# The inverse in an RWKV chunk loop: one factor by products, the other by 32x32 turns on VectorE

## What is computed

```python
def step(S, inp):
    r_t, w_t, k_t, v_t, kk_t, b_t = inp
    sa = jnp.einsum('bhvk,bhk->bhv', S, kk_t)
    S = (S * w_t[:, :, None, :] - sa[..., None] * b_t[:, :, None, :]
         + v_t[..., None] * k_t[:, :, None, :])
    return S, jnp.einsum('bhvk,bhk->bhv', S, r_t)
...
for d, reverse in enumerate((False, True)):
    ...
    yd_c, s_ctx = rwkv_scan(r_c, dec_c, k_c, v_c, kk_c, a_c, s0, reverse)
    yd, _ = rwkv_scan(r, dec, k_d, v, kk, a_d, s_ctx, reverse)
```

## Time and profile before

| | us |
|---|---|
| runs of the kernel before | 2665.66, 2661.81, 2665.49 |
| median | 2665.49 |
| profiled execution, its own time | 2672.74 |
| its span | 2671.0 |
| TensorE busy in the span | 2488.5 |
| VectorE / ScalarE / GpSimd busy | 1335.5 / 512.6 / 141.3 |

### The profile page before, as it was taken

The page is one execution under the profiler, slowest core; times in us unless marked ns, Lnnn a source line. Parts: engine busy times, 40 slices in busy tenths (PEclk is TensorE's granted clock), DMA queues, the critical chain, the costliest instruction groups (busy, mean ns, idle before and its releaser), DMA issues.

```text
span 2671.0 us, 49291 instructions
## 1 busy us (share of the span) xinstructions
PE 2488.5 (93%) x21560; PEld 1925.8 (72%) x21560; DVE 1335.5 (50%) x2478; ACT 512.6 (19%) x1032; POOL 141.3 (5%) x106
## 2 busy tenths in 40 slices
PE   8989999999999999999998989988887798999997
PEld 5945888888686548888884755457777746888786
DVE  4535555533454336555432365545665436787533
ACT  2122100101003320100001043323343222212100
POOL 0000000000000000000000000003223200000000
PEclk9988999999999999999999989998999998999998
DMA  5323322233221023222235102100000023222132
GB/s 165 119 79 126 95 71 88 75 87 107 64 66 62 1 77 113 95 79 70 77 93 160 48 16 66 51 1 4 5 4 4 4 95 119 71 95 95 48 88 71
DMA packets 221181, 190.53 MB, mean 71 GB/s; under 512 B 8727, under 2 KB 219064, under 8 KB 220968
## 3 DMA queue, kind: packets, MB, share of 16 engines
q1 hardware_dynamic: 220674, 187.29, 22.8%
q10 hardware_dynamic: 294, 0.09, 0.0%
HBM read 185.25 MB, written 2.10 MB: 70 GB/s over the span
## 4 chain that ended last, share of the span: by engine, by line
PE 86%; DVE 5%; issue 4%; ACT 1%; SPq 1%; POOL 1%; DMA 1%; DVEq 0%; POOLq 0%; ACTq 0%
PE psum L1630 30%; PE psum L1840 14%; PE psum L512 9%; PE psum L1130 4%; PE psum L2680 4%; PE psum L1344 3%; PE psum L2673 3%; PE psum L1341 3%; PE psum L3237 2%; PE psum L542 2%; PE psum L1066 1%; PE psum L2270 1%; PE psum L2252 1%; PE psum L1109 1%; PE psum L534 1%
## 5 line engine op out<-in xcount | busy, mean ns | idle before, releaser
L1630 PE MATMUL psum<-sbuf 128*128 128x256 f32 x3696 | 804.3, 381 | 4.0 <-DVE sbuf L476 1.9
L1630 PEld LDWEIGHTS psum<-sbuf 128*128 128x128 f32 x3696 | 704.7, 191 | 103.3 <-issue 3.2
L1840 PE MATMUL psum<-sbuf 128*128 128x256 f32 x1848 | 405.2, 382 | 11.1 <-DVE sbuf L1858 5.5
L1840 PEld LDWEIGHTS psum<-sbuf 128*128 128x128 f32 x1848 | 353.8, 192 | 62.1 <-DVE sbuf L1858 6.3
L1714 DVE TENSOR_TENSOR sbuf<-sbuf,psum 128x256 f32<-128x256 f32 x462 | 177.9, 417 | 200.5 <-PE psum L1630 199.3
L512 PE MATMUL psum<-sbuf 128*128 128x512 f32 (+3 forms) x688 | 248.1, 519 | 4.3 <-DVEq L617 4.0
L2680 PE MATMUL psum<-sbuf 64*64 64x64 f32 x4992 | 196.6, 225 | 40.3 <-issue 24.7
L512 PEld LDWEIGHTS psum<-sbuf 128*128 128x128 f32 (+2 forms) x688 | 129.6, 190 | 115.6 <-issue 103.4
L2680 PEld LDWEIGHTS psum<-sbuf 64*64 64x64 f32 x4992 | 170.6, 136 | 52.8 <-issue 43.9
L2673 PE MATMUL psum<-sbuf 64*64 64x64 f32 (+1 forms) x4544 | 176.1, 229 | 24.1 <-issue 17.9
L2673 PEld LDWEIGHTS psum<-sbuf 64*64 64x64 f32 x4544 | 158.6, 137 | 30.7 <-issue 21.5
(11 more groups left out here) (280 smaller groups left out, 2684.7 us busy)
## 6 DMA issues: line engine op xcount, KB each, us to landing
sbuf<-in_w_mod_dram SPq DMA_DIRECT2D x24, 1024.0 KB, 5.2
sbuf<-in_w_ffn_gate_dram SPq DMA_DIRECT2D x22, 1024.0 KB, 5.5
sbuf<-in_w_ffn_up_dram SPq DMA_DIRECT2D x22, 1024.0 KB, 7.6
sbuf<-in_w_ffn_down_dram SPq DMA_DIRECT2D x32, 704.0 KB, 6.0
sbuf<-in_w_up_dram SPq DMA_DIRECT2D x22, 1024.0 KB, 7.2
sbuf<-in_w_out_dram SPq DMA_DIRECT2D x12, 1024.0 KB, 8.1
sbuf<-in_w_in_dram SPq DMA_DIRECT2D x12, 1024.0 KB, 5.5
sbuf<-in_w_down_dram SPq DMA_DIRECT2D x16, 704.0 KB, 6.1
```

What stands on the lines that cost most here:

```text
L1630: mm = pe.matmul(bank, w[:, q, :], rhs[:, q, :], start=q == 0, stop=q == 3)
L1840: mm = pe.matmul(bank_of(g, p), wt[:, q, :], rhs_of[p][:, q, :], start=q == 0, stop=q == UNITS - 1)
```

## The change

`xy_level` no longer makes a new X. VectorE makes it from the new Y, by a turn of each 32x32 block in place (`turn_y`, two of 128x256 a level). X is only ever used for blocks of up to 32, so no block has to change places. Y now lies in the opposite half of the partitions, as the crosswise Gram product leaves it, and so do X and LOFF; hence `t_level` is by_head instead of crosswise. `gram_l` and `gram_lt` are gone: the crosswise part of the Gram product of b serves for the start value of Y (`y_init`) and for LOFF, and its straight part (by_head, with r, main chunks alone) goes to another bank. The order on VectorE, GpSimd and in the waits of TensorE follows.

```diff
-        def gram_l(g):
...
-                mm = by_head(pe, k.bank[7][:, column(p)], feature(AR, g, p // 4, p % 4)[:, 0, :], feature(B, g, p // 4, p % 4))
-        def gram_lt(g):
...
-                mm = crosswise(pe, k.bank[6][:, column(p)], feature(B, g, p // 4, p % 4), feature(AR, g, p // 4, p % 4)[:, 0, :])
         def gram(g, tile, signal):
-            if tile is B:
-                wait("y_init", g + 1)
-            else:
-                wait("gb", g + 1)
+            if tile is K:
+                wait("y_init", g + 1)
+                if main(g):
+                    wait("gb_out", g - NCH_CTX + 1)
+            else:
+                wait("prods", prep(g // 2, 1))
...
             for p in range(8):
...
+                if tile is K:
+                    mm = by_head(pe, k.bank[6 + p // 4][:, o:o + (P if main(g) else CH)], x, flat(rhs) if main(g) else rhs[:, 0, :])
+                else:
+                    mm = crosswise(pe, k.bank[6][:, column(p)], x, rhs[:, 0, :])
+                    if main(g):
+                        mm = by_head(pe, k.bank[7][:, column(p)], x, rhs[:, 1, :])
...
         def t_level(n, lv, aside):
...
-                    wait("xy", halves(n, lv - 1, d))
+                wait("x_done", halves(n, lv, d))
...
-                    mm = crosswise(pe, k.bank[2 * d][:, column(p % 4)], LOFF[lv][:, p, :], X[n % 2][:, p, :])
+                    mm = by_head(pe, k.bank[2 * d][:, column(p % 4)], LOFF[lv][:, p, :], X[n % 2][:, p, :])
...
         def xy_level(n, lv):
...
-                    if lv < LEVELS - 1:
-                        crosswise(pe, k.bank[2 * d + 1][:, column(p % 4)], Y[n % 2][:, p, :], T[:, p, :])
                     mm = by_head(pe, k.bank[2 * d][:, column(4 + p % 4)], T[:, p, :], Y[n % 2][:, p, :])
...
+        def turn_y(n, d):
+            dve.transpose(flat(X[n % 2][:, half(d), :]), flat(Y[n % 2][:, half(d), :])).then_inc(sems["x_done"], 1)
...
         def update(n, lv, d):
             wait("xy_done", halves(n, lv, d))
-            w = 2 if lv < LEVELS - 1 else 1
-            xy = XY[n % 2][:, 0:w, half(d), :].rearrange("p w f t -> p w (f t)")
...
+            y = flat(Y[n % 2][:, half(d), :])
+            dve.tensor_tensor(y, y, k.bank[2 * d][:, 256:512], ALU.subtract).then_inc(sems["xy"], 1)
+            if lv < LEVELS - 1:
+                wait("xy", halves(n, lv, d))
+                turn_y(n, d)
...
+                if lv == 3 and g < NCH:
+                    wait("gram_b", g + 1)
+                    evacuate_b(g, 0).then_inc(sems["gb"], 1)
...
                 if lv == 4 and g < NCH:
                     wait("gram_k", g + 1)
                     evacuate(g, GK, 0, 1)
+                    evacuate(g, GK, 1, 1).then_inc(sems["gk"], 1)
+                    wait("eye", g + 1)
+                    for d in range(2):
+                        turn_y(g, d)
                 if live:
                     update(n, lv, 0)
                 if lv == 3 and g < NCH:
-                    evacuate(g, GB, 1, 0).then_inc(sems["gb"], 1)
-                if lv == 4 and g < NCH:
-                    evacuate(g, GK, 1, 1).then_inc(sems["gk"], 1)
+                    y_init(g)
+                    if main(g):
+                        evacuate_b(g, 1).then_inc(sems["gb_out"], 1)
                 if live:
                     update(n, lv, 1)
...
-                wait("x_init", g + 1)
+                loff(g, 0)
                 wait("y_init", g + 1)
+                pool.tensor_tensor(Y[g % 2], Y[g % 2], mask(k, "eye", 0, CH).unsqueeze(1).broadcast_to([P, 8, CH]), ALU.add).then_inc(
+                    sems["eye"], 1)
                 if exps_in(n) is not None:
-                    wait("k_made", prep(exps_in(n), 1))
...
+                    wait("prods", prep(exps_in(n), 1))
+                for lv in range(1, LEVELS):
                     loff(g, lv)
```

More of the change, by code:

```diff
@@ L2704, in rwkv_loop @@
     sems = {n: k.sem(f"rwkv_{n}") for n in (
-        "latent_done", "rated", "cums_done", "exps", "k_gain", "kka", "k_made", "prods", "gram_l", "gram_lt", "gram_b", "gram_k", "x_init", "y_init",
+        "latent_done", "rated", "cums_done", "exps", "k_gain", "kka", "k_made", "prods", "gram_b", "gb_out", "gram_k", "y_init", "x_done",
         "gb", "gk", "loff", "eye", "t_done", "t_copied", "xy_done", "xy", "turned", "tok_copied", "kv_done", "kv_copied",
@@ L2782, in feature, with gram @@
             return tile[buf][d][:, f, c]
[L2784 to L2812 removed]
+        def gram(g, tile, signal):
+            if tile is K:
[4 more added lines that the diff above has]
+                wait("prods", prep(g // 2, 1))
+                if g == 1:
+                    wait("gk", 1)
+                elif g >= 2:
+                    wait("tok_copied", 3 * (g - 2) + 3)
+            for p in range(8):
+                x, rhs = feature(tile, g, p // 4, p % 4), feature(AR, g, p // 4, p % 4)
+                o = (p % 4) * P
+                if tile is K:
[4 more added lines that the diff above has]
+                        mm = by_head(pe, k.bank[7][:, column(p)], x, rhs[:, 1, :])
                 if p == 7:
@@ L2927, in tensor @@
                 aside = nothing
-                if lv == 1 and g < NCH:
-                    aside = gram_l(g)
-                elif lv == 2 and m >= 0:
+                if lv == 2 and m >= 0:
                     aside = outputs(m)
@@ L2955, in tensor @@
                     xy_level(n, lv)
-                if lv == 1 and g < NCH:
-                    gram_lt(g)
                 if lv == 2 and 0 <= m < NCH - 1:
@@ L3064, in products, with y_init, evacuate_b @@
             dve.tensor_tensor(Bf, rate, Bf, ALU.mult).then_inc(sems["prods"], 1)
-        def x_init(g):
-            wait("gram_l", g + 1)
-            dve.tensor_tensor(split(X[g % 2]), k.bank[7].rearrange("p (d f t) -> p d f t", d=2, f=4), both("x1", CH),
-                              ALU.mult).then_inc(sems["x_init"], 1)
-            wait("gram_lt", g + 1)
-            dve.tensor_tensor(split(Y[g % 2]), k.bank[6].rearrange("p (d f t) -> p d f t", d=2, f=4), both("y1", CH),
-                              ALU.mult).then_inc(sems["y_init"], 1)
+        def y_init(g):
+            dve.tensor_tensor(split(Y[g % 2]), k.bank[6].rearrange("p (d f t) -> p d f t", d=2, f=4), both("y1", CH), ALU.mult).then_inc(sems["y_init"], 1)
+        def turn_y(n, d):
+            dve.transpose(flat(X[n % 2][:, half(d), :]), flat(Y[n % 2][:, half(d), :])).then_inc(sems["x_done"], 1)
+        def evacuate_b(g, part):
+            mask_ = mask(k, "gram", part * CH, 7 * CH).rearrange("p (x w) -> p x w", w=CH)[:, 0::4, :].unsqueeze(2).broadcast_to([P, 2, 4, CH])
+            src_ = k.bank[6 + part].rearrange("p (d f t) -> p d f t", d=2, f=4)
+            return dve.tensor_tensor(split(GB[g % 2][:, :, part, :]), src_, mask_, ALU.mult)
         def evacuate(g, tile, d, slot):
@@ L3123, in vector @@
                     rate_products(exps_in(n))
-                if lv == 1 and g < NCH:
-                    x_init(g)
                 if lv == 1 and exps_in(n) is not None:
```

32 lines of the change are left out of this document (removed).

## The result

The changed kernel takes **2651.21 us** (median of 5 runs, 2649.75 to 2652.36), the kernel before 2665.49 beside it (5 runs, 2661.81 to 2671.13). The ratio is 0.9941, 95% interval 0.9927 to 0.9955: 0.6% faster, where 2666 was forecast. The profiled execution took 2651.21 (span 2649.4); that of before 2672.74 (span 2671.0), so the two profiles differ by 21.5, the medians by 14.3.

What follows compares the result with a forecast made beforehand. TensorE was taken as the bound, though idle a fifth of the stretch, mostly for instructions. Path +24.4, start -4.1 and blocks -21.3 summed to -1.0 us from 2665.5, rounded up to 2666; range 2648 to 2685.

Steps and rivals of the forecast that it cites:

- The path, +24.4: TensorE's path through all twelve chunks: changed waits and paces at each level add 24.4 us in sum.
- The turn at 0.42: VectorE's turn of 128x256 in SBUF: taken as 0.42 us, with bounds 0.27 + 0.05 and 0.69.
- The wait ahead of the gram of k: Levels 3 to 4: update, turn and evacuations delay TensorE 2.48 us after xy_level's first half, against 1.63 before.
- TensorE's waits for VectorE: In the loop: grow from 11 to over 35 us, most of it ahead of the gram of k.
- The start, -4.1: Ahead of chunk 0: gram_l and gram_lt, run alone at the lower clock level, go, saving 4.1 us.
- The blocks, -21.3: Instruction blocks in the loop: 16 fewer at 0.58 us save 9.3, cheaper gaps on the other 67 save 12.
- the other 67 at 0.40: Remaining instruction blocks: gap taken as 0.40 us each instead of 0.58, saving 12 us; bounds 0.2 and 0.58.
- The sign of being wrong: Main chunks' length: the prediction is wrong if they leave 30 us by more than 1.5 either way.
- The fetch gives back more: Faster rival: gaps fall to 0.2 us a block, 13 us more, and a shorter turn up to 9; 2650, chance 0.20.
- The gaps that stay: Slower rival: instruction gaps keep the same total, so the path's +24.4 - 4.1 stands alone; 2686, chance 0.12.
- The port: Slower rival: VectorE's turns are delayed by GpSimd's operations through a shared port, 15 us; 2681 to 2682, chance 0.15.
- The clock as a rival of 100 us: Slower rival: clock falls in the more often idle loop, records 52 ns not 30, over 100 us; chance next to nothing.

Runs made afterwards that it cites:

- 768 products: Changed kernel with the old X's 768 crosswise products put back into xy_level at levels 0 to 3, unread; 2670.29 us, ratio to before 1.0018.
- The narrow run: Changed kernel with the 768 crosswise X products put back unread, each over 8 columns instead of 64; 2674.83 us, ratio to before 1.0035.
- the fill version: Changed kernel with the turns of v moved ahead of level 1's first products and two heads' outputs ahead of level 2's; 2645.36 us, ratio to before 0.9928.

## Why the prediction was wrong, step by step

**Removed instructions: right.** 82 packets became 66, 16 fewer.

**The path, +24.4: right in sum.** All that is not "issue" grew by 21.9 us in the loop. The clock's shortfall is in it with 0.6 (2.1 against 1.5).

- Outputs at one helper's pace: right. 222 records in 6.69 us, 29 ns each as taken from the earlier trace rows.
- The turn at 0.42: it takes 0.44, inside the bounds from the earlier trace rows. The estimate worked out from the figure in the Trainium skill, "VectorE: DVE Perf Modes", section "The three transpose paths" (311 ns for 128x128 in bf16), was 0.44; the trace agrees with the estimate, and no run here has the shape and type that the Trainium skill gives.
- The wait ahead of the gram of k, 2.48 us forecast after the first half of `xy_level`. In chunk 9, against the earlier trace rows, VectorE's queue is the one in the sum, row by row:

```profile
2064.49 0.69 DVE L3056 TENSOR_TENSOR sbuf<-psum,sbuf 128x512 f32<-128x512 f32 x1 [0.38 <-PE psum L2673]
2065.10 0.41 DVE L3067 TENSOR_TENSOR sbuf<-sbuf,psum 128x256 f32<-128x256 f32 x1
2065.55 0.45 DVE L3051 STREAM_TRANSPOSE sbuf<-sbuf 128x256 f32<-128x256 f32 x1
2065.92 0.65 DVE L3048 TENSOR_TENSOR sbuf<-psum,sbuf 128x512 f32<-128x512 f32 x1
2066.49 0.67 DVE L3056 TENSOR_TENSOR sbuf<-psum,sbuf 128x512 f32<-128x512 f32 x1
```

```profile
2066.14 0.33 PE L2673 MATMUL psum<-sbuf 64*64 64x64 f32 x4 [0.65 <-DVE sbuf L3051]
2067.32 3.71 PE L2673 MATMUL psum<-sbuf 64*64 64x128 f32 x92 [0.84 <-DVE sbuf L3056]
2072.55 0.65 PE L2673 MATMUL psum<-sbuf 64*64 64x64 f32 x15 [1.52 <-DVE sbuf L3067]
```

  From `update` (2065.10) to TensorE's return (2067.32) it is 2.22 us; the sum had 2.48 less 0.29 for the same, 2.19.
- TensorE's waits for VectorE, over 35 us forecast: 38.6, from the rows above and three small ones. That most of it would lie ahead of the gram of k was wrong; the turns hold 22.2 in 36 places (L3051), the gram of k 6.7 in eight (L3056). Even with the 0.65 for the turn of level 3 just ahead of it, as in chunk 9 above, the place comes to an estimated 12 (8 x 1.49).

**The start, -4.1: right.** ScalarE's first copy of T came at 1820.47 before and at 1818.54 after, 1.9 earlier, though the loop's first Gram product was 2.2 later (1807.37 in the earlier trace rows, 1809.57 after; the part ahead of the loop ended later in this execution). Together 4.1.

**The blocks, -21.3: the step that failed.** The 16 blocks that went were worth 9, as reckoned. The mis-sized term is "the other 67 at 0.40": 66 blocks measured 0.10 each, and (0.56 - 0.10) x 66 is 30 us, where 12 stood. With -39.8 in place of -21.3 and everything else as forecast, the sum is -19.5; the two profiles differ by -21.5. Carried over to the median it gives 2646, where 2651.2 was measured, so this term is more than the whole distance, and what makes up the 5 us the other way is not shown (before's profiled execution lies 7.2 above its median, the changed kernel's at it). Besides, 2664.5 was rounded up to 2666 with no row behind the 1.5.

The reason given, that slower work hides a gap, pointed the right way. But the price was fitted to the pace close by a gap, with `kv` and `sa` left dense and therefore charged. The runs show that such dense work costs little where slower work surrounds it (6.4 us in all, 12.0 once it is brought together), and that the other work per packet, which went from 3.29 to 4.41 us, decides most. The lower bound of 0.2 was too high for the same reason.

**The sign of being wrong came.** Main chunks were to stay within 1.5 us of 30. By the copy of the earlier trace rows, the four from 1940.33 to 2050.37 us took 26.7, 26.6, 30.2 and 26.6, the same four before 28.9, 28.6, 30.0 and 30.1. One of these copies after:

```profile
1966.99 0.60 ACT L2985 ACTIVATE sbuf<-psum 128x512 f32<-128x512 f32 x1 [1.40 <-PE psum L2680]
```

**The rivals.** "The fetch gives back more", chance 0.20 at 2650, is what happened, in kind. That its number was so near is partly luck: it had 0.2 a block, 13 us more from the blocks where the loop's rows show some 18 more, and besides a shorter turn, 0.32, which was not so. "The gaps that stay" fell with 46 to 6 us (its own 2686 lay outside the stated range). The port fell as well. GpSimd's operations run from 2050.21 for 4.96 us (four of L3132), and the turns beside them, at 2051.38 and 2052.16, are no longer than the one at 2060.75 with GpSimd idle:

```profile
2051.38 0.45 DVE L3051 STREAM_TRANSPOSE sbuf<-sbuf 128x256 f32<-128x256 f32 x1
...
2052.16 0.45 DVE L3051 STREAM_TRANSPOSE sbuf<-sbuf 128x256 f32<-128x256 f32 x1
...
2060.75 0.45 DVE L3051 STREAM_TRANSPOSE sbuf<-sbuf 128x256 f32<-128x256 f32 x1
```

The clock as a rival of 100 us did not come; in small it did, as told below.

**The rule on blocks.** The Trainium skill, "Runtime: NRT & Kernel Launch", section "Instruction fetch mechanics", says crossing a block is mostly hidden. By the rows it depends on the load: 0.56 us a block before, 0.10 after. The same section of the Trainium skill gives TensorE room for 128 KiB of instructions, eight such blocks, filled ahead in order. A stock would fit the smoothing seen above, but the traces do not show one of eight: 255 for each packet started, less the TensorE instructions started, varies over the loop by some 250 before and 180 after, about one packet.

What remains open: of the 19 us that 768 products cost, 18.3 are "issue" rows, but in the profiles the whole stretch grew by 22.2; 7.4 us more count as TensorE busy, and 4.4 fewer as waits for VectorE and GpSimd. Whether TensorE's small gaps inside busy rows are fetches too was not taken apart. The narrow run doesn't separate fetching an instruction from handling it there either. Why packets keep 3.2 us or more apart is open.

## What to carry to other kernels

Where a TensorE loop of small products shows "issue" waits, divide the packets of the instruction queue into the time of all other work. In this loop, below some 4 us of other work a packet, a removed product is worth more than its own time, and a slower but shorter instruction stream can win; above it, instructions are cheap as long as dense stretches stand apart, and the waits for other engines are the next thing to read. Then look which side of a wait covers it: the turns of v and two heads' products moved into a wait gave 6 us, while moving everything gave nothing. A single queue (VectorE's) that holds both a recurrence's update and evacuations for later is best ordered by who waits first.

## What the runs showed of the hardware

- Instructions for TensorE came in packets of 255, never less than 3.2 us apart, and all 299 "issue" waits ended 2.15 to 2.97 us after a packet's start. Gaps followed the work per packet as in the table. A product of 8 columns cost as much as one of 64 (2674.8 against 2670.3 us for 768 of them).
- VectorE's turn of 128x256 fp32 in 32x32 blocks takes 0.44 us, about as long as an arithmetic operation of that size (0.42, L3095 in the earlier trace rows); GpSimd beside it changed nothing in the two turns shown (0.45).
- TensorE's granted clock falls in short stretches inside a loop that is over 80% busy. In the fill version, 5.5 us behind a stretch of waits (0.64 us busy in 2) ran at a mean of 0.69, a mix of the two levels, with 92 records at about 56 ns that elsewhere take 38:

```profile
2057.00:2059.00 2.00, 0.64 (x16) 0.39 (x10) 1.97 (x5) 0.00 (x0) 1.81 (x2) 1.00 0.02 4
2059.00:2064.50 5.50, 5.34 (x92) 5.23 (x92) 1.68 (x4) 0.77 (x2) 5.50 (x5) 0.69 0.01 3
```

  One such fall costs 1.7 us (5.5 x 0.31). The profiles had between none and about four of them, which is as much as the smaller moves were worth. What sets them off is not settled.
